# A decoder layer with 32 experts on one core: 4 KB weight rows for narrow experts, a class of width 120, the gate's clip on ScalarE, the last activation ahead of the last weight split

## What is computed

```
logits = xt @ w_router + b_router                  # 1024 x 32
top_vals, top_idx = top_k(logits, 4); gates = softmax(top_vals)
per expert e, on the rows of its tokens:
  gu = x_e @ w_gate_up[e] + b_gate_up[e]           # 1024 -> 2 x 1024
  g = min(gu[:, :1024], 7);  u = clip(gu[:, 1024:], -7, 7)
  act = (u + 1) * (g * sigmoid(1.702 * g))
  y_e = act @ w_down[e] + b_down[e]                # 1024 -> 1024
out[token] += gate * y_e
```

## Time and profile before

| | us |
|---|---|
| median of 3 runs (lowest, highest) | 1879.18 (1879.03, 1880.25) |
| the profiled execution's own time | 1882.29 |
| its span | 1880.5 |
| TensorE, VectorE, ScalarE, GpSimd busy | 1800.9, 1402.1, 1231.7, 411.4 |
| DMA traffic | 479.07 MB, 255 GB/s on average |
| mean granted TensorE clock | 0.982 |

### The profile page before, as it was taken

One profiled execution on the slowest core, in us unless ns is written; L12 is line 12 of the kernel. 1 busy time (PEld: TensorE's weight loads), 2 busy tenths in 40 slices (PEclk: granted clock), 3 DMA queues, 4 the chain that ended last, 5 costly groups with the idle time before them and its releaser, 6 DMA issues.

```text
span 1880.5 us, 53844 instructions
## 1 busy us (share of the span) xinstructions
PE 1800.9 (96%) x21814; PEld 1650.7 (88%) x21814; DVE 1402.1 (75%) x2678; ACT 1231.7 (65%) x1649; POOL 411.4 (22%) x304
## 2 busy tenths in 40 slices
PE   8999998998987999999999999999999999999996
PEld 7777765666876999999999999999999999999996
DVE  5553637775258888888888899999889877757755
ACT  6565327873114777777777788877777776656654
POOL 4000000001003212111112332333122224434433
PEclk9999999999988999999999999999999999999998
DMA  5211101004438988889999999999999999999994
GB/s 153 56 44 39 30 24 45 2 1 142 142 120 295 369 293 308 304 302 320 325 320 322 328 313 343 344 336 345 373 375 365 372 372 374 377 375 372 362 370 134
DMA packets 251408, 479.07 MB, mean 255 GB/s; under 512 B 17312, under 2 KB 38096, under 8 KB 251264
## 3 DMA queue, kind: packets, MB, share of 16 engines
q1 hardware_dynamic: 231040, 443.59, 64.9%
q0 software_dynamic: 20256, 33.94, 7.6%
HBM read 466.96 MB, written 47.19 MB: 273 GB/s over the span
## 4 chain that ended last, share of the span: by engine, by line
PE 50%; issue 6%; DVE 6%; ACT 4%; DMA 2%; DVEq 0%; SPq 0%; POOLq 0%; ACTq 0%; POOL 0%
PE E_p_d L2254 9%; PE E_p_g L2242 5%; PE E_p_g L2245 5%; PE E_p_g L2244 5%; PE E_p_u L2242 5%; PE E_p_u L2245 5%; PE E_p_u L2244 5%; PE E_p_d L2242 3%; PE E_p_d L2245 3%; PE E_p_d L2244 3%; DVE E_w_lo L1996 3%; DMA E_w_st<-in_w_down 2%; PE E_p_t L2180 2%; PE E_p_t L2195 2%; ACT E_w_hi L1869 2%
## 5 line engine op out<-in xcount | busy, mean ns | idle before, releaser
L1996 DVE SCALAR_TENSOR_TENSOR E_w_lo<-E_w_st,E_w_hi 128x2048 f16<-128x2048 f32 x336 | 767.2, 2283 | 31.7 <-ACT E_w_hi L1869 30.5
L1869 ACT ACTIVATE E_w_hi<-E_w_st 128x2048 f16<-128x2048 f32 x336 | 639.0, 1907 | 20.3 <-PEq L1325 16.8
L2242 PE MATMUL E_p_u<-E_x_hi,E_w_hi 128*128 128x128 f16 (+9 forms) x2048 | 366.9, 222 | 1.5 <-DVE E_w_lo L1996 1.4
L2244 PE MATMUL E_p_g<-E_x_lo,E_w_hi 128*128 128x128 f16 (+9 forms) x2048 | 366.9, 222 | 0.5 <-issue 0.5
L2242 PE MATMUL E_p_g<-E_x_hi,E_w_hi 128*128 128x128 f16 (+9 forms) x2048 | 366.9, 222 | 0.0
L2245 PE MATMUL E_p_g<-E_x_hi,E_w_lo 128*128 128x128 f16 (+9 forms) x2048 | 366.9, 222 | 0.0
L2245 PE MATMUL E_p_u<-E_x_hi,E_w_lo 128*128 128x128 f16 (+9 forms) x2048 | 366.8, 222 | 0.0
L2244 PE MATMUL E_p_u<-E_x_lo,E_w_hi 128*128 128x128 f16 (+9 forms) x2048 | 366.8, 222 | 0.0
L1799 POOL DMA_INDIRECT out<-E_y_rows,E_idx_out x66 | 152.6, 2312 | 488.0 <-ACT E_y_rows L1887 467.1
L2242 PE MATMUL E_p_d<-E_a_hi,E_w_hi 128*128 128x160 f16 (+6 forms) x1024 | 210.6, 231 | 6.9 <-DVE E_a_lo L2090 3.5
L2245 PE MATMUL E_p_d<-E_a_hi,E_w_lo 128*128 128x160 f16 (+6 forms) x1024 | 210.5, 231 | 0.0
(11 more groups left out here) (419 smaller groups left out, 3487.2 us busy)
## 6 DMA issues: line engine op xcount, KB each, us to landing
E_w_st<-in_w_gate_up SPq DMA_DIRECT2D x130, 2048.0 KB, 13.5
E_w_st<-in_w_down SPq DMA_DIRECT2D x64, 2048.0 KB, 18.7
A_w_st<-in_w_in SPq DMA_DIRECT2D x20, 512.0 KB, 4.0
A_x_rows<-in_x SPq DMA_DIRECT2D x8, 512.0 KB, 7.9
C_x_res<-in_x SPq DMA_DIRECT2D x8, 512.0 KB, 4.7
x_rows<-C_x SPq DMA_DIRECT2D x8, 512.0 KB, 5.2
out<-C_x SPq DMA_DIRECT2D x8, 512.0 KB, 5.9
h_rows<-C_h SPq DMA_DIRECT2D x8, 512.0 KB, 4.5
```

Source lines behind the costliest of these rows:

```text
L1869: act.activation(w_hi[r][:], staged(c), ACT.Copy, scale=SW).then_inc(hi_s if c < NG else down_hi_s, 1)
L1996: dve.scalar_tensor_tensor(out=w_lo[r][:], in0=staged(c), scalar=SW, in1=w_hi[r][:], op0=ALU.mult, op1=ALU.subtract, accum_out=total[:, c: ...
L2242: pe.matmul(o_, wh, hi[:, k, 0:w], start=h == 0 and k == 0, stop=False, skip_group_check=True)
L2244: pe.matmul(o_, wh, lo[:, k, 0:w], start=False, stop=False, skip_group_check=True)
```

## The change

Six parts.

1. `WIDTHS` gets a class of 120 between 128 and 112. Items of 113 to 120 tokens, so far in class 128, now have bodies of their own.
2. In classes below 128 (`long(w)`) two of the four down chunks, 2 and 3, are split and 0 and 1 are whole; the ring has six buffers there too, and the next item's first four chunks are split during the down chunks, as in the wide items. The order of the eight first chunks becomes four gate chunks, then four up chunks.
3. The weights lie in three slots of 4 MB (gate or mixed, up or mixed, down), each filled by two requests. In narrow items a request takes 512 rows by 1024 columns (`rows_of`), so in rows of 4 KB; wide items keep 512 columns of all rows (`columns_of`), 2 KB.
4. SP's order in narrow items: both up requests after the fourth up split, both down requests after `down_free_s` (ScalarE signals it at the second down chunk, ahead of that chunk's y_bias), then both gate requests for item i+2. The last two wide items form the passage. GpSimd works out the borders (`ends`) in stage D.
5. The gate's clip moves from VectorE to ScalarE, as a Relu with a turned sign (LIMIT minus the gate, not below zero), and Silu turns it back with scale and bias. The up clip stays on VectorE.
6. In step c = 7 of the wide classes ScalarE makes the last `activated_hi` ahead of the split of chunk 11, and VectorE the last `activated_lo` ahead of its half.

```diff
-WIDTHS = (256, 192, 184, 176, 168, 160, 152, 144, 136, 128, 112, 96)
+WIDTHS = (256, 192, 184, 176, 168, 160, 152, 144, 136, 128, 120, 112, 96)
...
+def rows_of(a, e, q):
+    r = slice(q % 2 * D // 2, (q % 2 + 1) * D // 2)
+    if q < 4:
+        src = a.w_gate_up[0][bass.ds(e, 1), r, q // 2 * D:(q // 2 + 1) * D]
+    else:
+        src = a.w_down[0][bass.ds(e, 1), r, :]
+    return src.rearrange("o (k p) n -> p (o k) n", p=P)
+def by_rows(w_st, q):
+    return w_st[q // 2][:, q % 2 * KT // 2:(q % 2 + 1) * KT // 2, :]
+IN_TURN = (0, 2, 1, 3)
...
+        def split_down(w):
+            if not fast:
+                return ()
+            return range(NP) if w > SLIM else range(NP // 2, NP) if long(w) else range(NP // 2)
+        def chunk_of(c, w):
+            if long(w):
+                return c < NP, c % NP
+            return c % 2 == 0, c // 2
...
+                    def behind(lo, hi, down_free, per_item):
+                        with sp.If(hi > lo):
+                            with sp.Fori(lo, hi) as i:
+                                e_next = expert(sp, i + 1)
+                                load_up(i, e_next, True)
+                                sp.wait_ge(down_free, per_item * i + per_item)
+                                for q in range(4, 6):
+                                    load(e_next, q, True)
+                                load_later(i, True)
...
+                    among_wide(ends[0], ends[1], True)
+                    behind(ends[1], ends[2], down_lo_s, NP)
+                    behind(ends[2], n_items - 1, down_free_s, 1)
...
                     def silu(j):
+                        act.wait_ge(gu_mm, NG * i + c + 1)
+                        if j >= 2 and not long(w):
+                            act.wait_ge(act_s if fast else a_s, NP * i + j - 1)
+                        for h in range(2):
+                            ins = act.activation(gate_of(j, w)[:, h, :], bank_of(c, w)[:, h, 0:w], ACT.Relu,
+                                                 bias=bias[:, f + h:f + h + 1], scale=-1.0)
+                        ins.then_inc(gate_s, 1)
                         act.wait_ge(gate_s, FREE + NP * i + j + 1)
-                        act.activation(gate[j % 2][:, :, 0:w], gate[j % 2][:, :, 0:w], ACT.Silu, scale=ALPHA / S1
-                                       ).then_inc(silu_s, 1)
+                        act.activation(gate_of(j, w), gate_of(j, w), ACT.Silu, scale=-ALPHA / S1,
+                                       bias=top[:]).then_inc(silu_s, 1)
...
+                        if fast and j == (1 if long(w) else NP - 1):
+                            act.wait_ge(down_lo_s, NP * i + NP)
+                            act.sem_inc(down_free_s, 1)
...
+                            if not long(w) and c == NG - 1:
+                                activated_hi(c // 2)
+                            if cc < NG or cc - NG in split_down(w):
+                                staged_sy(act, cc, i + 1, w)
+                                split_hi(cc, ring(cc))
...
-                    def clip_gate(j):
...
+                            if not long(w) and c == NG - 1:
+                                activated_lo(j)
+                            if cc < NG:
+                                split_lo(NG * i + cc + 1, cc, ring(cc))
+                            elif cc - NG in split_down(w):
+                                split_lo(NP * i + cc - NG + 1, cc, ring(cc))
```

341 lines of the change are left out of this document (191 added, 150 removed).

## The result

| | before | changed |
|---|---|---|
| median (lowest, highest), six runs each on one chip, us | 1879.72 (1877.44, 1885.08) | 1888.03 (1885.20, 1891.99) |
| the profiled execution's own time, us | 1882.29 | 1888.99 |
| its span, us | 1880.5 | 1887.2 |
| mean granted TensorE clock | 0.982 | 0.980 |

The ratio is 1.0040, with an interval of 1.0022 to 1.0059. The forecast was 1861 us in a range of 1848 to 1873 and faster; the change made the kernel 0.4% slower.

What follows compares the result with a forecast made beforehand. Narrow items stood against TensorE, queues and the VectorE chain at once, wide ones against TensorE alone, except at 136. Narrow −28.9, wide +10.8, rest −0.3: −18.4, from the median 1861 us, range 1848 to 1873.

Steps and rivals of the forecast that it cites:

- Class 120: Three items moved from class 128 to 120 gain 1.6 us each in TensorE's split chunks: −4.7 us.
- The queues' floor: Narrow items: 4 KB rows at 413 GB/s bring weights to 30.5 us, items to 33.9 at 112, 33.2 at 96.
- the rest of the period, 3.4 us at 112 and 2.7 at 96, is what gather and scatter take: Narrow items' queues: period beyond the weights' 32.4 us, added to the new 30.5 us for the floor.
- The vector engines' loop: Narrow items: ScalarE's chain, VectorE's split and TensorE up to the chain's start close a loop of 32.3 us.
- rival C: ScalarE's chain is longer, 34.5 us at 112 and 96; 1874 us; sign: TensorE waits for w_lo at 112; chance 0.15.
- B: Rival: 4 KB rows are no faster, queues hold 112 and 96 where they are; slower, 1886 us; chance 0.10.
- Wide items, 152 and above: a_hi before the last split makes x_lo late for TensorE, 0.8 us per item of 160: +7.1 us.
- 144 and 136: Five items lose 2.3 us each behind the order, gain 1.6 from three clips: +0.7 each, +3.7 us.
- At 144 and 136 VectorE is already the pace: Step crediting three clips taken from VectorE in these items: 0.53 us each, −1.6 per item.
- Rival A: Wide items don't pay: x_lo still comes before TensorE, waits of 136 and 144 vanish; about −35, 1844 us; chance 0.15.
- The clock: TensorE's granted clock: nothing in the change makes TensorE idle longer, so no term was given.
- The last item: The final item, of width 96, gains 2.5 us: −2.5.

Runs made afterwards that it cites:

- both faults put right: Changed kernel with the last activation behind the last split again and the second down slot requested before the gate halves, above 128: 1861.67 us, ratio 0.9894 to the kernel before.

## Why the prediction was wrong

**Class 120.** −4.7 forecast, and 128 and 120 together gave −5.0 against −5.1. That the sum fits so well is partly luck. TensorE does set the second and third item of 120, it has no wait there but one of 0.3 us; but they start 34.7 us apart and not 35.2, so they gained 2.1 each where 1.6 was sized, and the first, with a wait of 0.9 us for y_t, took 36.45 and gained 0.3. With half of the down weights left out that first one took 35.5.

**The queues' floor.** This is the step that failed first, for 112 and 96. The rate was right: rows of 4 KB gave 410 GB/s against 413 forecast, 30.7 us for the weights. In the run that changes nothing else, 4 KB rows beat 2 KB rows by 1.7 us per item, so rows of 2 KB were not yet at the highest rate. The Trainium skill ("DMA: Bandwidth & Descriptors", Specifications) asks for at least 512 B for line rate; by that rule the two would have been equal, and the measurement decides. What failed was "the rest of the period, 3.4 us at 112 and 2.7 at 96, is what gather and scatter take". At 96 the period of 35.15 was not the queues' own: less than an item's weights came in it. By the bytes the rest is 36.0 − 32.4 = 3.6 us, and it is 34.3 − 30.7 = 3.6 in the changed kernel too. The floor was 34.3 and not 33.2. At 112, where the period before was the queues' own pace, it was 34.5 on average where 33.9 was worked out. Then I went below my own floor (33.5 and 32.7) because the new order of requests was to give slack; only the first item of each class had any (33.1 us each, by TensorE's first matmuls).

**The vector engines' loop.** Sized 32.3 us, with the narrow queues relieved it measured 33.0 at 96 and 33.6 at 112, and 31.8 at 96 without the clip. So rival C's mechanism is real, but in this kernel it is hidden: moving the clip away changes nothing while the queues are full. Its figure, 34.5, came close for another reason. Even its sign was there, TensorE waiting for w_lo of an up chunk (2.0 us over the five items of 112, 7.2 over the four of 96), so that wait does not tell the two apart. B fell with the 410 GB/s; the slower total came without it.

**Wide items, 152 and above.** The mechanism was right in each of its steps, the size a little low: +9.7 against +7.1 (0.94 per item at 160 for 0.8, and 1.2 for 184 and 176 together where 0.2 was sized).

**144 and 136.** +12.1 against +3.7. The forecast was +2.3 per item for the order and −1.6 for the clips, so +11.5 and −8. The runs gave +13.4 for the order (214.9 against 201.5) and −1.3 for the clips (201.5 against 202.8). So the larger error is the clips' credit, and behind it the step "At 144 and 136 VectorE is already the pace": with both faults put right the items take 198.2, 0.9 each below the kernel before, and TensorE is then busy for 39.65 us of an item of 144 that takes 39.85, where it took 40.6 before. So about 0.8 us was to be had there before TensorE set the pace, and part of that was held up by the second down slot, which was already late without part 6: putting it first returned 3.3 us there and 6.0 behind the new order. The forecast followed what is queued behind the new wait on SP in the narrow items, and not SP in the wide ones. Rival A, that the wide items would not pay, is refuted there and at 160.

**The clock.** "Nothing in the change makes TensorE idle longer than it does now, so no term is for the clock" failed, and against the prediction's own terms, since it has TensorE wait for x_lo in every wide item. The waits for x_lo at 144 and 136 were 13.1 us in all, and behind three of them the granted clock fell: 0.97 over the five items, up to 7 us of TensorE's time by the estimate above. In the five kernels with the old order (the kernel before and four of the experiments) it was 1.00 there. So that the order's +13.4 lies near the forecast's +11.5 is partly luck: up to half of it is a term that the forecast had put at nothing.

**The last item.** −2.5 forecast, +1.6 measured. I took only TensorE's saving. The splits for the next item had moved to where the last item has nothing behind them to hide: 5.9 us of them came off when they were left out.

**The rest.** The item stage began 1.5 us earlier than in the profiled execution of before. No experiment isolates it, and the starts of all traces scatter by 6 us. The clock goes with it: the three traces that began at 594.2 to 594.4 had a mean granted clock of 0.97 up to there, the ten others, from 597.1 on, 0.95 or 0.96.

What stays open: how the loss at 144 and 136 divides between the wait for x_lo, the clock behind it and the late slot. No run holds one of them and takes away another. In the changed kernel and the six experiments that keep both its order and its clips in these items, the sum of these items goes with the clock, 208.9 at 0.99, 212.8 to 213.8 at 0.98, 214.9 and 215.0 at 0.97, 218.2 at 0.95, but a longer wait can be the cause of both. That gather and scatter take 3.6 us per item is measured as a difference, not by taking them away.

## What to carry to other kernels

A period in which a queue never rests is not yet that queue's pace: compare the bytes that came with the bytes that the period needs, since the difference is drawn from what was fetched ahead. When a step is moved behind another, follow what it releases as far as the next transfer's request, and look at the last turn of the loop, where the work that used to hide it is missing. Work that is taken from an engine is worth no more than what the next limit leaves: 1.6 us of clips per item returned 0.3. A wait that is filled on a third engine can come back under another name. And where a change makes TensorE wait, look at the granted clock behind the wait before you say that it has no term.
